# Hybrid decoder trunk, gated linear attention: ScalarE's two level copies move ahead of the next chunk's decays

## The chip, the core and the metric

One core of a Trainium2 chip runs the whole program. The time is the device time of one execution, in microseconds (us); three executions of the kernel before gave 2348.33, 2348.94 and 2350.07 us, so the median is 2348.94 us.

The core has five engines that run side by side, each with its own instruction list, worked off in order. TensorE (PE in the profile) multiplies matrices and writes to PSUM; VectorE (DVE) and ScalarE (ACT) read and write SBUF and PSUM; GpSimd (POOL) works on SBUF here; SyncE (SP) issues the transfers. They meet by semaphores: an instruction that waits holds up everything behind it on its own engine.

## The reference

Two layers. Each layer normalises x, projects it to the inputs of four mixers and a gate, runs the mixers, multiplies by SiLU(gate), projects back and adds to x. SEQ is 1024 and D_MODEL 1024. The change is inside mixer A, gated linear attention (GLA), with 8 heads, 32 key channels and 64 value channels a head:

```python
def step(S, inp):
    q_, k_, v_, g_ = inp
    G = jnp.cumsum(g_, axis=2)
    o_inter = jnp.einsum('bhtk,bhkv->bhtv', q_ * jnp.exp(G), S)
    diff = G[:, :, :, None, :] - G[:, :, None, :, :]
    decay = jnp.exp(jnp.where(causal, diff, -jnp.inf))
    A = jnp.sum(q_[:, :, :, None, :] * k_[:, :, None, :, :] * decay, axis=-1)
    o = o_inter + jnp.einsum('bhts,bhsv->bhtv', A, v_)
    G_last = G[:, :, -1:, :]
    S_new = jnp.exp(G_last[:, :, 0, :])[..., None] * S + jnp.einsum('bhsk,bhsv->bhkv', k_ * jnp.exp(G_last - G), v_)
    return S_new, o
```

The output o then gets an RMSNorm over each head's 64 channels. The scores A inside a chunk carry a decay for each key channel, so they are no plain product of q and k.

## The kernel before

**Tiling of the mixer.** The kernel works in 8 chunks of 128 tokens (TT = 8). The 128x128 causal triangle of a chunk is cut in 7 levels: level 1 is the one 64x64 block below the diagonal, level 2 the two 32x32 blocks, and so on to 64 blocks of one element at level 7; the diagonal itself comes from a plain product of k and q. Within a level a block's decay splits into a factor for the keys and one for the queries, both exponentials of differences to G at the block's edge. The levels go in three batches, (1, 2), (3, 4, 5) and (6, 7) (`BATCHES`).

**What each engine does for chunk c** (a step that I call mix c, c = 0 to 7):

- VectorE, `mix_dve`: `exponent(c + 1)`, 14 subtractions (lines 737 and 738) that write the exponents of the next chunk into one of the two halves of the buffer gla_E; then `mask_batch(c, 0)`, whose one instruction (line 787) writes the diagonal, and with it all of gla_A, after it has waited for the output of chunk c - 1 (`out_done`); `state(c - 1)` (lines 823 and 826); `means(c - 1)` (lines 832 and 833), which waits for ScalarE's squares; `mask_batch(c, 1)`, three masked copies (line 797) of levels 3 to 5; `normalise(c - 1)` (line 837); `mask_batch(c, 2)`, two masked copies (line 797) of levels 6 and 7.
- ScalarE, `mix_act`: `copy_k_end(c - 1)` (line 880); `decay(c + 1)`, four exponentials (lines 862, 865 and twice 867) that wait for `exponent(c + 1)` and release GpSimd's products of the next chunk; `move_level(c, 1)` and `move_level(c, 2)`, three plain copies in all (line 809) from PSUM into gla_A, which wait for line 787 (the semaphore `masked`) and count up the semaphore `moved`; `square(c - 1)` (line 886); `root(c - 1)` (lines 890 and 891), which waits for the means.
- TensorE, `mix_pe`: `scores(c, 0)` (lines 767 and 774), which waits for all of chunk c - 1's masked copies; `finish(c - 1)` (lines 916, 924, 927 and 937), the output and the state of the chunk before; `scores(c, 1)` (line 774, 48 matmuls), which waits for `moved` of this chunk, since its results go over the same PSUM columns; `scores(c, 2)` (line 774, 32 matmuls), which waits for the masked copies of levels 3 to 5. After each of the three parts stand 10 matmuls (line 255) of other projections, put there by `units_between`.
- GpSimd, `chunk_pool(c + 1)` in the time of mix c: after `decay(c + 1)` it multiplies q and k with the decays (lines 707 and 709), batch by batch, and each batch first waits until TensorE has done the same batch of chunk c (`scored`); line 724 makes the last two products. In chunks 0, 1, 3, 4, 6 and 7 it also does a quarter of a weight tile's low part (line 209) after the second batch and another one at the end.

All orders are written out by hand; there is no planner. After mix 7 TensorE goes on with the gate projections of the same mixer. `scalar_gla` calls `mix_act` for c = 0 to 7, with evacuations of the projections in between, once in each layer.

Of the kernel before, what the change touches and what calls it, by code (L numbers as in the profile page):

```python
# [559 lines left out]
class Gla:  # L560
# [332 lines left out]
    def mix_act(self, act, link, c):  # L893
        if c >= 1:
            self.copy_k_end(act, c - 1)
        if c + 1 < TT:
            self.decay(act, c + 1)
        self.move_level(act, c, 1)
        self.move_level(act, c, 2)
        if c >= 1:  # L900
            self.square(act, c - 1)
            self.root(act, link, c - 1)
# [2096 lines left out]
```

## Time and profile before

| what | value |
|---|---|
| median of three executions | 2348.94 us |
| the profiled execution's own time | 2350.63 us |
| its span in the profile | 2348.8 us |
| TensorE busy | 2266.7 us (97%) |
| VectorE busy | 1130.9 us (48%) |
| GpSimd busy | 920.6 us (39%) |
| ScalarE busy | 895.8 us (38%) |
| the eight mixes of layer 0 | about 118 to 248 us of the span |
| the eight mixes of layer 1 | about 1280 to 1411 us of the span |

Busy time is the sum of an engine's instructions. The chain of waits follows the work that ended last back through what released it. A row of the timeline gives start, duration, engine, line, operation, output<-inputs, shapes and count; in square brackets stands how long the engine was idle before it, and what ended the idle time.

### The profile page before, as it was taken

How to read it: one execution, taken by the hardware profiler on the slowest of the kernel's cores; microseconds unless marked ns; L12 is line 12 of the kernel's file. 1: busy time of each engine (PE TensorE's matmuls, PEld its weight loads, DVE VectorE, ACT ScalarE, POOL GpSimd, SP SyncE). 2: the span in 40 equal slices, each digit the busy share in tenths (PEclk: the TensorE clock that was granted, in tenths of full speed). 3: DMA queues.
4: the chain of work that ended last, by engine and by line, in shares of the span. 5: the costliest groups of instructions: out<-in, count | busy, mean ns of one | idle time of the engine just before them, and what ended most of it. 6: DMA issues, size and time to landing. Idle time of an engine off the chain costs nothing.

```text
span 2348.8 us, 35114 instructions
## 1 busy us (share of the span) xinstructions
PE 2266.7 (97%) x14164; PEld 1737.2 (74%) x14164; DVE 1130.9 (48%) x2214; ACT 895.8 (38%) x1496; POOL 920.6 (39%) x978
## 2 busy tenths in 40 slices
PE   7989999999999999999999899999999999999999
PEld 7877888986595785655697778889866958866556
DVE  4377243634427225767433771446153371277763
ACT  5333225613424433353443332156143343344441
POOL 2166113223724511565433542122245245017563
PEclk9999999999999999999999999999999999999999
DMA  4100232240100111300421003322301001122003
GB/s 158 41 20 20 91 112 90 73 144 1 36 20 1 52 48 65 135 1 1 145 73 40 20 20 91 137 65 90 126 1 37 19 1 52 59 78 111 1 1 135
DMA packets 92018, 141.30 MB, mean 60 GB/s; under 512 B 18352, under 2 KB 65488, under 8 KB 91856
## 3 DMA queue, kind: packets, MB, share of 16 engines
q1 hardware_dynamic: 91856, 139.05, 17.3%
q8 instruction: 113, 1.85, 0.3%
q14 instruction: 49, 0.40, 0.1%
HBM read 105.48 MB, written 33.55 MB: 59 GB/s over the span
## 4 chain that ended last, share of the span: by engine, by line
PE 86%; DVE 9%; ACT 3%; issue 2%; POOL 0%; DMA 0%; SPq 0%; ACTq 0%; DVEq 0%
PE psum L255 40%; PE psum L524 15%; PE psum L1442 6%; PE psum L1425 4%; PE psum L1404 3%; PE psum L1430 3%; PE psum L1428 3%; PE psum L1390 3%; PE psum L774 2%; DVE gla_A L797 2%; PE psum L1449 1%; DVE gla_E L737 1%; PE psum L1042 1%; PE psum L1828 1%; DVE mla_nm L1563 1%
## 5 line engine op out<-in xcount | busy, mean ns | idle before, releaser
L209 POOL TENSOR_TENSOR w_lo<-w_raw,w_hi 128x512 fp32r<-128x512 f32 (+3 forms) x240 | 320.3, 1360 | 757.0 <-ACT w_hi L194 757.0
L255 PE MATMUL psum<-h_hi,w_hi 128*128 128x512 f32 x768 | 203.9, 406 | 0.0
L255 PE MATMUL psum<-h_hi,w_lo 128*128 128x512 f32 x768 | 196.8, 396 | 0.0
L255 PE MATMUL psum<-h_lo,w_hi 128*128 128x512 f32 x768 | 195.2, 394 | 0.0
L194 ACT ACTIVATE w_hi<-w_raw 128x2048 fp32r<-128x2048 f32 (+2 forms) x64 | 114.5, 1788 | 184.1 <-PE psum L524 161.7
L255 PE MATMUL psum<-w_hi,h_hi 128*128 128x256 f32 (+3 forms) x1280 | 183.6, 286 | 0.0
L1637 POOL TENSOR_TENSOR mla_acc<-mla_acc,mla_p 128x512 f32<-128x512 f32 (+3 forms) x160 | 153.5, 977 | 74.1 <-ACT mla_p L1496 74.1
L255 PE MATMUL psum<-w_lo,h_hi 128*128 128x256 f32 (+3 forms) x1280 | 179.4, 283 | 0.0
L255 PE MATMUL psum<-w_hi,h_lo 128*128 128x256 f32 (+3 forms) x1280 | 179.4, 283 | 0.0
L1637 POOL TENSOR_TENSOR fox_acc<-fox_acc,fox_p 128x512 f32<-128x512 f32 (+3 forms) x160 | 150.7, 960 | 73.1 <-ACT fox_p L1496 72.7
L255 PEld LDWEIGHTS psum<-w_hi,h_hi 128*128 128x128 f32 x1280 | 165.4, 192 | 6.0 <-issue 5.8
L255 PEld LDWEIGHTS psum<-h_hi,w_hi 128*128 128x128 f32 x768 | 143.5, 193 | 32.4 <-issue 3.0
L255 PEld LDWEIGHTS psum<-h_hi,w_lo 128*128 128x128 f32 x768 | 144.6, 190 | 30.9
L255 PEld LDWEIGHTS psum<-h_lo,w_hi 128*128 128x128 f32 x768 | 143.7, 189 | 31.0
L255 PEld LDWEIGHTS psum<-w_lo,h_hi 128*128 128x128 f32 x1280 | 164.7, 191 | 0.1
L255 PEld LDWEIGHTS psum<-w_hi,h_lo 128*128 128x128 f32 x1280 | 164.7, 191 | 0.0
L1496 ACT ACTIVATE mla_p<-psum 128x512 f32<-128x512 f32 (+1 forms) x192 | 93.9, 490 | 153.5 <-PE psum L1432 115.7
L1496 ACT ACTIVATE fox_p<-psum 128x512 f32<-128x512 f32 (+1 forms) x192 | 94.2, 490 | 152.4 <-PE psum L1432 114.3
L557 DVE TENSOR_TENSOR x_rows<-x_rows,psum 128x512 f32<-128x512 f32 x128 | 86.0, 686 | 130.4 <-PE psum L524 103.9
L707 POOL TENSOR_TENSOR gla_E<-gla_kT,gla_E 128x128 f32<-128x128 f32 x112 | 54.0, 482 | 151.0 <-ACT gla_kT L643 66.9
L797 DVE COPY_PREDICATED gla_A<-gla_masks,psum 128x512 f32<-128x512 int32 x80 | 77.4, 968 | 30.0 <-PE psum L774 27.5
L1404 PE MATMUL psum<-mla_k,mla_q 128*128 128x512 f32 (+1 forms) x192 | 73.9, 422 | 11.8 <-DVE mla_nm L1567 7.5
(333 smaller groups left out, 4426.2 us busy)
## 6 DMA issues: line engine op xcount, KB each, us to landing
w_raw<-in_w_in_dram SPq DMA_DIRECT2D x38, 1024.0 KB, 5.4
out_dram<-x_rows SPq DMA_DIRECT2D x64, 512.0 KB, 2.7
x_rows<-out_dram SPq DMA_DIRECT2D x56, 512.0 KB, 5.3
w_raw<-in_w_out_dram SPq DMA_DIRECT2D x16, 1024.0 KB, 6.3
x_first<-in_x_dram SPq DMA_DIRECT2D x8, 512.0 KB, 7.3
x_rows<-in_x_dram SPq DMA_DIRECT2D x8, 512.0 KB, 5.3
w_raw<-in_w_in_dram SPq DMA_DIRECT2D x2, 1088.0 KB, 10.0
w_raw<-in_w_in_dram SPq DMA_DIRECT2D x2, 1056.0 KB, 5.1
```

What stands on the lines that cost most here:

```text
L194: last = act.activation(self.w_hi[c["set"]][:, at], self.w_raw[c["set"]][:, at], ACT.Copy)
L209: last = pool.tensor_tensor(self.w_lo[c["set"]][:, at], self.w_raw[c["set"]][:, at], self.w_hi[c["set"]][:, at].bitcast(F32), ALU.subtract)
L255: last = pe.matmul(o, lhs, rhs, start=(kk == 0 and n == 0), stop=(kk == KT - 1 and n == 2))
L524: last = pe.matmul(k.bank(u), y, w[:, c, :], start=(c == 0 and i == 0), stop=(c == CT - 1 and i == 2))
L557: dve.tensor_tensor(at, at, ps, ALU.add).then_inc(k.evac_sem["dve"], 1)
L797: dve.copy_predicated(self.halves(self.A[:, :, :], level)[:, :, :, 1, :], m, ps).then_inc(self.masked.sem, 1)
L1390: last = pe.transpose(k.psum[:D, self.misc_bank("pre", p, g), x * P:(x + 1) * P], src(a, 4 * c + x), k.ident[:, :])
L1404: pe.matmul(out, q[:, a, x * P:(x + 1) * P], kk[:, a, :hi - lo], start=True, stop=True).then_inc(self.scores.sem, 1)
L1425: pe.matmul(out, self.k_hi[ks][:, a, keys], self.q_lo[qs][:, a, lo:], start=True, stop=False)
L1442: pe.matmul(self.k.psum[a * HEAD:(a + 1) * HEAD, 4 + i % 2, lo:], self.pairs[p]["v"](a, kb), self.p[:, u % self.PR, lo:], start=(kb == 0), ...
L1496: act.activation(self.p[:, u % self.PR, lo:], self.k.psum[:, u % 2, lo:], ACT.Exp).then_inc(self.exp_done.sem, 1)
L1637: pool.tensor_tensor(acc, acc, p, ALU.add).then_inc(self.acc_done.sem, 1)
```

## The change

Three calls of `mix_act` change places. For every chunk, `move_level(c, 1)` and `move_level(c, 2)` now stand ahead of `decay(c + 1)` in ScalarE's list. No instruction is added or taken away, no wait changes its condition, and the other engines' lists stay as they are.

```diff
     def mix_act(self, act, link, c):
         if c >= 1:
             self.copy_k_end(act, c - 1)
+        self.move_level(act, c, 1)
+        self.move_level(act, c, 2)
         if c + 1 < TT:
             self.decay(act, c + 1)
-        self.move_level(act, c, 1)
-        self.move_level(act, c, 2)
         if c >= 1:
             self.square(act, c - 1)
             self.root(act, link, c - 1)
```

## Rows read from the trace of the kernel before

**Rows 1.** The page's chain of waits: shares of the span by line.

```profile
PE psum L255 40%; PE psum L524 15%; PE psum L1442 6%; PE psum L1425 4%; PE psum L1404 3%; PE psum L1430 3%; PE psum L1428 3%; PE psum L1390 3%; PE psum L774 2%; DVE gla_A L797 2%; PE psum L1449 1%; DVE gla_E L737 1%; PE psum L1042 1%; PE psum L1828 1%; DVE mla_nm L1563 1%
```

**Rows 2.** Windows: stretch, length, busy (count) PE, PEld, DVE, ACT, POOL; clock, DMA.

```profile
100.00:256.00 156.00, 143.33 (x1647) 117.89 (x1646) 107.65 (x221) 53.57 (x106) 76.45 (x140) 0.98 0.05 15
256.00:560.00 304.00, 304.00 (x1607) 256.57 (x1606) 114.94 (x147) 110.84 (x141) 80.35 (x59) 1.00 0.29 98
1262.00:1419.00 157.00, 145.86 (x1648) 119.66 (x1647) 107.22 (x221) 53.87 (x106) 76.39 (x140) 0.97 0.05 15
1419.00:1700.00 281.00, 281.00 (x1491) 237.64 (x1491) 106.16 (x117) 104.88 (x132) 68.30 (x51) 1.00 0.31 106
```

**Rows 3.** Timeline of ScalarE in mix 3, layer 0, and the next mix's first decay.

```profile
173.40 1.70 ACT L862 ACTIVATE gla_E<-gla_E 128x1792 f32<-128x1792 f32 x1 [2.19 <-DVE gla_E L738]
...
175.31 0.68 ACT L867 ACTIVATE gla_E<-gla_G,gla_end 128x128 f32<-128x128 f32 x2
175.90 1.22 ACT L809 ACTIVATE gla_A<-psum 64x512 f32<-64x512 f32 x3
177.15 0.60 ACT L886 ACTIVATE gla_v<-psum 128x512 f32<-128x512 f32 x1
...
189.66 1.71 ACT L862 ACTIVATE gla_E<-gla_E 128x1792 f32<-128x1792 f32 x1 [2.16 <-DVE gla_E L738]
```

**Rows 4.** Timeline of VectorE in mix 3.

```profile
173.50 1.23 DVE L787 TENSOR_TENSOR gla_A<-psum,ident 128x1024 f32<-128x1024 f32 x1
...
177.78 0.69 DVE L832 TENSOR_REDUCE gla_ms<-gla_v 128x8 f32<-128x512 f32 x1 [1.94 <-ACT gla_v L886]
...
178.81 2.23 DVE L797 COPY_PREDICATED gla_A<-gla_masks,psum 128x512 f32<-128x512 int32 x3
...
182.37 2.72 DVE L797 COPY_PREDICATED gla_A<-gla_masks,psum 128x512 f32<-128x512 int32 x2 [0.75 <-PE psum L774]
```

**Rows 5.** Timeline of TensorE in mix 3: the second and third batch of scores.

```profile
177.17 1.57 PE L774 MATMUL psum<-gla_ql,gla_E 32*128 32x64 f32 x48 [0.93 <-ACT gla_A L809]
...
181.18 1.12 PE L774 MATMUL psum<-gla_ql,gla_E 32*128 32x64 f32 x32
```

**Rows 6.** Timeline of GpSimd in mix 3: starts of batches 1 and 2, both weight quarters.

```profile
176.12 0.46 POOL L707 TENSOR_TENSOR gla_E<-gla_kT,gla_E 128x128 f32<-128x128 f32 x1 [5.13 <-ACT gla_E L867]
...
178.85 0.47 POOL L707 TENSOR_TENSOR gla_E<-gla_kT,gla_E 128x128 f32<-128x128 f32 x1 [1.03 <-PE psum L774]
...
181.35 1.27 POOL L209 TENSOR_TENSOR w_lo<-w_raw,w_hi 128x512 fp32r<-128x512 f32 x1
...
185.94 1.31 POOL L209 TENSOR_TENSOR w_lo<-w_raw,w_hi 128x512 fp32r<-128x512 f32 x1
```

**Rows 7.** Timeline of VectorE and GpSimd at the end of mix 0.

```profile
130.02 6.89 DVE L737 TENSOR_TENSOR gla_E<-gla_G 128x128 f32<-128x128 f32 x1
...
135.44 1.32 POOL L209 TENSOR_TENSOR w_lo<-w_raw,w_hi 128x512 fp32r<-128x512 f32 x1
```

**Rows 8.** Timeline of VectorE and ScalarE in mix 2.

```profile
158.24 1.23 DVE L787 TENSOR_TENSOR gla_A<-psum,ident 128x1024 f32<-128x1024 f32 x1 [1.38 <-PE psum L927]
...
159.50 1.24 ACT L809 ACTIVATE gla_A<-psum 64x512 f32<-64x512 f32 x3
...
162.55 2.25 DVE L797 COPY_PREDICATED gla_A<-gla_masks,psum 128x512 f32<-128x512 int32 x3 [0.26 <-PE psum L774]
```

**Rows 9.** Timeline of TensorE and VectorE in mix 1.

```profile
143.34 2.84 PE L774 MATMUL psum<-gla_ql,gla_E 32*128 32x64 f32 x48 [5.68 <-ACT gla_A L809]
...
146.25 2.26 DVE L797 COPY_PREDICATED gla_A<-gla_masks,psum 128x512 f32<-128x512 int32 x3 [1.41 <-PE psum L774]
...
149.65 1.12 PE L774 MATMUL psum<-gla_ql,gla_E 32*128 32x64 f32 x32
```

**Rows 10.** Windows: a stretch of mix 1; columns as in rows 2.

```profile
144.00:150.00 6.00, 6.00 (x66) 4.92 (x66) 3.57 (x6) 1.06 (x3) 2.55 (x6) 0.64 0.00 0
```

**Rows 11.** Timeline of GpSimd in mix 4: start of the third batch.

```profile
198.67 0.53 POOL L707 TENSOR_TENSOR gla_E<-gla_kT,gla_E 128x128 f32<-128x128 f32 x1 [1.02 <-PE psum L774]
```

## Prediction, made before the changed kernel ran

> **What bounds the kernel now.** I read the page's chain first: it is TensorE nearly throughout, and only at the GLA lines do others appear, DVE L797 with 2% and DVE L737 with 1% of the span [rows 1]. So whatever a mix of GLA loses, TensorE loses. The windows say the same and how much room there is. In the 156 us around the eight mixes of layer 0 TensorE is busy for 143.33, so it stands for 12.7 us; in layer 1 for 157 - 145.86 = 11.1; in the stretches that follow (304 and 281 us) it is busy for all of it [rows 2]. A delay of the last mix is therefore carried to the end of the kernel one to one, and a gain too, up to those 24 us.
>
> Then I read one mix of each kind as a timeline. Mix 3 is the regular one. Call T the start of its first decay, 173.40; the next one starts at 189.66, a period of 16.26 us [rows 3]. The chain through it is:
> - decays T to T+2.59 (the last ends at 175.31 + 0.68), moves to T+3.72, squares T+3.75 to T+4.35 [rows 3];
> - second batch of scores on TensorE from T+3.77 to T+5.34, after 0.93 us idle for the moves; third batch from T+7.8 to T+8.9 [rows 5];
> - GpSimd starts batch 1 with the decays at T+2.72, is done with it at 177.82, waits 1.03 us for the second scores, starts batch 2 at T+5.45, and from there to the end of its second weight quarter (185.94 + 1.31 = 187.25, T+13.85) it never stops: 8.40 us [rows 6];
> - VectorE ends its last masked copy at 182.37 + 2.72 = T+11.69 [rows 4], but the 14 subtractions that follow are done only at about 189.6: 2.4 us after GpSimd's last instruction. That VectorE stands still while GpSimd runs is plain in mix 0: a subtraction that takes 0.28 elsewhere took 6.89 us, from 130.02 to 136.91, and GpSimd's last quarter ended at 136.76 [rows 7].
>
> So the period is 5.45 + 8.40 + 2.41 = 16.26: decays, moves, second scores, GpSimd's unbroken stream, rest of the subtractions.
>
> **The change, part by part.** It removes no work. It puts 1.22 us of moves ahead of 2.59 us of decays [rows 3]. Two things come earlier or later by that.
>
> *Moves.* They need line 787, which runs 173.50 to 174.73 [rows 4], so they can start at T+1.37 and end at T+2.6 where they now end at T+3.72. TensorE was idle only from 176.24 (177.17 - 0.93), so the second scores start at T+2.9 and are 0.9 us earlier; they end at T+4.45.
>
> *Decays.* They now run T+2.6 to T+5.2, 2.6 later. Behind them on ScalarE stand the squares, to T+5.8 (1.45 later), and the root. Released by them are GpSimd's next chunk and, through the squares, VectorE's means, and both are in front of what sets the period:
> - GpSimd: start T+5.3 (0.13 after the decays, as now); batch 1 takes 177.82 - 176.12 = 1.7, to T+7.0. The second scores are long there, so it doesn't wait, and the same 8.40 us end at T+15.4 instead of T+13.85. Rest of the subtractions 2.4: next T at T+17.8. Period +1.5.
> - VectorE: means from T+5.85 to T+6.75 (177.78 to about 178.67 now, 0.9), masked copies of batch 1 (2.23) to T+9.0; third scores T+9.1 to T+10.2 (now T+7.8 to T+8.9, TensorE waits some 2.15 us before them); last masked copies end at T+12.95 instead of T+11.69. That is +1.25 by itself.
>
> The 0.9 us that the scores gain is used by nobody: masked copies of batch 1 stand behind the means, GpSimd's batch 2 behind its late batch 1.
>
> By mix:
> - Mix 0: line 787 is the later of the two conditions now too; the moves stay where they are, and the decays, 3.8 us later, are done before GpSimd has finished chunk 0. 0.
> - Mix 1: the one gain. TensorE has been idle for 5.68 us at 143.34 for the moves [rows 9], and starts 1.3 earlier (2.59 of decays less 1.23 of line 787 and its hop). Means end at about 146.15, as late as the 146.25 at which the masked copies start now, so these hardly move; the third scores, at 149.65 now behind ten matmuls at a lowered clock, are then bound by 146.2 + 2.25, at 148.5. -1.2.
> - Mix 2 and mix 5: line 787 waited 1.38 us for the output matmuls and ended at 159.47 = X; the moves start at 159.50 either way, since the decays lay wholly beside that wait [rows 8]. Here nothing is earlier, and the decays move from before X to X+1.27 to X+3.87. Squares to X+4.5, means to X+5.4; masked copies start then instead of at 162.55 = X+3.08: +2.35 on VectorE's path. GpSimd: batch 1 to X+5.65 where batch 2 starts at X+3.1 now, +2.5 to its end. +2.5 each.
> - Mix 3: +1.5 as above.
> - Mix 4: GpSimd has no quarters and already waits 1.02 us for the third scores [rows 11]; it starts later with a stop less, and the third scores' +1.25 counts. +1.25.
> - Mix 6: no subtractions follow; VectorE's last masked copy opens the next scores. +1.25.
> - Mix 7: no decays, 0, and it passes on what it gets.
>
> Sum for a layer: -1.2 + 2.5 + 1.5 + 1.25 + 2.5 + 1.25 = +7.8. Layer 1 has the same lists and nearly the same windows [rows 2]; I take +7.6 there, since TensorE's wait in its mix 1 is a little different. Total +15.4. On the profiled execution's own time: 2350.63 + 15.4 = 2366.0. That execution lies 1.7 us over the median of the runs shown, so in their terms 2348.94 + 15.4 = **2364.3 us**.
>
> *What the trace does not show, from both sides.* How much of the subtractions slips in while GpSimd runs. Now three of 14 do, at the joints of its last instructions; the late stream meets VectorE at the same offset (12.95 against 15.4, before 11.69 against 13.85), so I keep 2.4. If all 14 wait, as the first one did for 6.89 us [rows 7], that is 0.6 more in the three mixes of a layer that follow a stream with quarters: +3.6 in all; if GpSimd never held VectorE, only VectorE's own +1.25 and +2.35 count, and the sum is 7.5 a layer at most, less 0.3 to 1. The Trainium skill ("SBUF — State Buffer", section "Who interferes with whom") says that a VectorE instruction with two SBUF inputs and a GpSimd instruction that reads SBUF exclude each other, and that the one holding the port keeps it for its whole instruction. The trace agrees that they exclude each other; but 6.89 us is many GpSimd instructions of 0.46 to 1.3 us, so the hold here can last a whole stream. By the page's unit, the end of an instruction, the sum would stay at +15.4; by the long hold it is +19.
>
> The other unknown is TensorE's clock. After the idle 5.68 us of mix 1 the granted clock of 144 to 150 us was 0.64, and 48 matmuls took 2.84 us where they take 1.57 at the full 2.4 GHz [rows 5, 9, 10]. After gaps of 0.93 it did not fall. The new order makes gaps of 2.15 us before the third scores in five mixes a layer. From nothing to about 1 us each (1.12 us of scores at half clock) is +0 to +10; I take 0, nearer to the 0.93 row. In mix 1 the gap shrinks to 4.3 us, which may save a microsecond.
>
> **The rivals.**
> - *The early scores pay, and the decays hide* (faster). If GpSimd's idle 5.13 us before a chunk were real slack and the squares cost nothing, mixes 3, 4 and 6 would gain 0.93 each and mix 1 1.2: 4.0 a layer, 2348.9 - 8 = 2341. For it: TensorE waits for the moves in the chain. Against it: GpSimd's stream runs unbroken into the subtractions [rows 6], and the squares are behind the decays on the one list. It decides at whether batch 2 on GpSimd (T+5.45) starts later than now.
> - *It evens out* (within the noise): gains in mixes 1, 3, 4, 6 against losses of mixes 2 and 5 only: -8 + 10 = +2, 2351. It needs the regular mixes to gain, against the same two rows.
> - *Worse than the sum*: the long hold, with some lowered clocks: +19 to +25, 2368 to 2374.
>
> **How the numbers follow.** Forecast 0.76; worse than the sum 0.14; evens out 0.04; faster 0.06. This kernel's runs tell a difference of about 0.2%, 4.7 us, from none. Slower 0.90, same 0.04, faster 0.06. Range: the forecast's own bounds are about +12 (VectorE's path alone, a better mix 1) to +19; with part of the worse case +23: 2358 to 2372.
>
> **What would show it.** In the changed profile the moves (L809) end before L862 starts; scores x48 start about 2.9 us after the subtractions; GpSimd's first L707 of a chunk comes 5.3 us after them, with no stop before batch 2; L832 starts 1.4 to 2.6 later and L797 x3 directly behind it; periods near 17.8 for mix 3, 16.3 for mix 4; the eight mixes end near 256 instead of 248 us; TensorE is 8 us longer idle in each layer, with gaps in front of L774 x32 released by L797. If L862 after mix 3 comes 16.3 us or less after the one before, the prediction is wrong.

## The result, and the profile after

The changed kernel took 2382.91 us, median of four executions (2379.53 to 2390.78), against 2348.74 us before: the ratio is 1.0149, 95% interval 1.0124 to 1.0175. Slower, as forecast, but by 34 us where I had said 15.4, and outside my range (2358 to 2372). Timed once more beside the last experiment it gave 1.0146 (1.0127 to 1.0165).

The profiled execution has a span of 2377.7 us, 28.9 more than before. First the windows of the changed kernel that answer to [rows 2] (stretch, length, busy and count of PE, PEld, DVE, ACT, POOL, then granted clock, DMA share, GB/s):

```profile
150.00:263.00 113.00, 101.26 (x1182) 82.33 (x1181) 73.53 (x144) 35.19 (x72) 49.84 (x92) 0.89 0.04 11
263.00:290.00 27.00, 27.00 (x133) 22.68 (x132) 3.62 (x6) 8.08 (x11) 5.03 (x4) 1.00 0.53 157
290.00:560.00 270.00, 270.00 (x1443) 228.63 (x1442) 104.47 (x114) 99.67 (x126) 69.98 (x52) 1.00 0.27 95
```

After the mixes TensorE is busy without a stop, as before. But inside them the granted clock has a mean of 0.89, where it was 0.98 over the whole of that stage [rows 2], and 1.00 in mixes 2 to 6 alone (150 to 238 us of the kernel before). That is new, and it is where the missing time is. Mix 3 of the changed kernel, timeline of ScalarE (answers to [rows 3]):

```profile
176.26 1.24 ACT L809 ACTIVATE gla_A<-psum 64x512 f32<-64x512 f32 x3 [3.54 <-DVE gla_A L787]
177.52 1.70 ACT L862 ACTIVATE gla_E<-gla_E 128x1792 f32<-128x1792 f32 x1
179.43 0.68 ACT L867 ACTIVATE gla_E<-gla_G,gla_end 128x128 f32<-128x128 f32 x2
180.14 0.60 ACT L886 ACTIVATE gla_v<-psum 128x512 f32<-128x512 f32 x1
```

VectorE (answers to [rows 4]) and TensorE (to [rows 5]) in the same mix:

```profile
175.00 1.22 DVE L787 TENSOR_TENSOR gla_A<-psum,ident 128x1024 f32<-128x1024 f32 x1 [0.88 <-PE psum L927]
180.77 0.69 DVE L832 TENSOR_REDUCE gla_ms<-gla_v 128x8 f32<-128x512 f32 x1 [3.44 <-ACT gla_v L886]
181.57 2.18 DVE L797 COPY_PREDICATED gla_A<-gla_masks,psum 128x512 f32<-128x512 int32 x3
177.72 1.57 PE L774 MATMUL psum<-gla_ql,gla_E 32*128 32x64 f32 x48
183.81 1.78 PE L774 MATMUL psum<-gla_ql,gla_E 32*128 32x64 f32 x32 [2.02 <-DVE gla_A L797]
191.01 1.01 PE L774 MATMUL psum<-gla_ql,gla_E 32*128 32x64 f32 x32
```

Read it from the top: line 787 ends at 176.22, the moves follow at once, the decays, the squares, and VectorE's means wait 3.44 us for the squares. The three masked copies start only behind the means, though their scores were done at 179.3. TensorE has then waited 2.02 us ahead of the third scores, and from there it is slow: 1.78 us for the 32 matmuls, and the chain of waits shows the ten matmuls of other projections (line 255, called the product matmuls from here on) on the path behind them, at nearly twice their usual 2.5 us:

```profile
183.81 1.78 PE psum L774 x32
185.59 4.56 PE psum L255 x10
190.16 1.02 PE psum L767 x16
```

From the start of the third scores to the start of the next mix's x32 it is 191.01 - 183.81 = 7.20 us. In the kernel before it was 4.51 in the same mix, from 181.18 [rows 5] to this row of its timeline:

```profile
185.69 1.02 PE L774 MATMUL psum<-gla_ql,gla_E 32*128 32x64 f32 x32
```

That interval is a good gauge of the clock, since where the granted clock is 1.00 it is 4.5 us. In mixes 2 to 6 of the changed kernel it is 5.63, 7.20, 5.67, 5.65 and 7.21 in layer 0, and 5.67, 4.50, 5.65, 7.21 and 5.66 in layer 1. What lies over 4.5 adds to 8.9 + 6.2 = 15.1 us. The span grew by 28.9; without that it would have grown by 13.8, where the sum was 15.4. Counted from line 787 of mix 0 to line 787 of mix 7, the mixes of the two layers took 117.8 and 118.5 us before and take 134.2 and 132.0 now: 29.9 more, and 14.8 without the 15.1.

Mix 1 stands apart. TensorE waits less there than before, 2.94 us instead of 5.68, and the 48 matmuls run at full speed; the eight product matmuls behind them, which take 2.0 us elsewhere, are slow all the same, and the granted clock of 141 to 147 us is 0.72:

```profile
141.04 1.57 PE L774 MATMUL psum<-gla_ql,gla_E 32*128 32x64 f32 x48 [2.94 <-ACT gla_A L809]
142.53 3.30 PE L255 MATMUL psum<-h_hi,w_lo 128*128 128x512 f32 x8
```

That fall costs little, since the third scores wait for the masked copies there anyway, by 0.92 us. It shows that a first row at full speed does not yet mean a full clock.

### The profile page after: what moved, and what is told of

Its sections match the earlier page's. It is cut to its first block, busy times and chain, and to the rows that moved or that the text cites. A ratio compares the mean times of both kernels' runs of the same rounds, so it can differ in the third digit from the quotient of the medians.

```text
span 2377.7 us, 35114 instructions
## 1 busy us (share of the span) xinstructions
PE 2283.8 (96%) x14164; PEld 1749.4 (74%) x14164; DVE 1131.7 (48%) x2214; ACT 896.4 (38%) x1496; POOL 917.6 (39%) x978
## 4 chain that ended last, share of the span: by engine, by line
PE 84%; DVE 9%; ACT 4%; issue 2%; POOL 0%; DMA 0%; SPq 0%; DVEq 0%; ACTq 0%
PE psum L255 39%; PE psum L524 15%; PE psum L1442 6%; PE psum L1425 4%; PE psum L1404 3%; PE psum L1430 3%; PE psum L1428 3%; PE psum L1390 3%; DVE gla_A L797 2%; PE psum L774 2%; PE psum L1449 1%; PE psum L1042 1%; PE psum L1828 1%; PE psum L927 1%; DVE mla_nm L1563 1%
## 5 line engine op out<-in xcount | busy, mean ns | idle before, releaser
L255 PE MATMUL psum<-h_lo,w_hi 128*128 128x512 f32 x768 | 202.3, 404 | 0.0
L774 PE MATMUL psum<-gla_ql,gla_E 32*128 32x64 f32 x1792 | 62.4, 281 | 32.9 <-DVE gla_A L797 24.7
L774 PEld LDWEIGHTS psum<-gla_ql,gla_E 32*128 32x128 f32 x1792 | 57.2, 195 | 46.2 <-DVE gla_A L797 31.5
```

What stands on the lines that cost most here:

```text
L255: last = pe.matmul(o, lhs, rhs, start=(kk == 0 and n == 0), stop=(kk == KT - 1 and n == 2))
L774: last = pe.matmul(out[:, i, g, :], self.E[r, c % 2, level - 1, g, :], self.ql[r, level - 1, g, :], start=True, stop=True)
```

## The experiments

Ratios are to the kernel before on the same chip in the same rounds. Its median was 2347.95 us beside four of the kernels (after filled, squares first, squares late, after with quarters moved), 2351.66 beside the next four (after filled in mixes 2 to 6, before with quarters moved, split decays, squares first with quarters moved) and 2349.27 beside the last two.

**After, filled.** TensorE gets something to do in the wait:

```diff
         between(pe, 1)
+        if 1 <= c < TT - 1:
+            name, part = unit_between(BETWEEN * (self.NBATCH * c + 2) // UNIT_MATMULS)
+            bank = self.k.bank(self.k.u(self.layer, name, *part))
+            for i in range(8):
+                pe.matmul(bank[:64, :P], self.k.upper[64:, :64], self.k.ident[64:, :], start=False, stop=False,
+                          skip_group_check=True)
         self.scores(pe, c, 2)
```

> The changed kernel, with 8 matmuls more in mixes 1 to 6 on TensorE, right ahead of the third batch of scores. They multiply zeros into the open accumulation of the projection that runs there (64 rows, 64x128 of it), so nothing that is computed changes; at about 0.21 us each they fill 1.7 of the 2.0 us that TensorE waits there in the changed kernel. Theory A (clock): that wait drops TensorE to its lower clock, and the scores (1.78 us for 32 matmuls where 1.12 is usual) and the ten product matmuls behind (4.56 where 2.5 is usual) are on the path. Then the filling gives the time back: 2364 to 2368 us, the granted clock of 150 to 260 us near 1.0 instead of 0.89. Theory B (something else makes these matmuls slow, or the serial chain of diagonal, moves, decays, squares, means and masks alone costs the 34 us): no change or slower, 2380 to 2390 us.

Measured: 2369.42 us, ratio 1.0086 (1.0069 to 1.0103), against the changed kernel's 1.0149: more work on TensorE, and some 13 us less. Its mix 3:

```profile
183.74 1.96 PE L952 MATMUL psum<-ident,upper 64*64 64x128 f32 x16
186.31 1.12 PE L774 MATMUL psum<-gla_ql,gla_E 32*128 32x64 f32 x32 [0.61 <-DVE gla_A L797]
190.83 1.02 PE L774 MATMUL psum<-gla_ql,gla_E 32*128 32x64 f32 x32
```

The interval is 4.52 again in this mix, and 4.5 in eight of the ten (mix 6 of both layers has 5.64); the granted clock of 150 to 250 us is 0.98 instead of 0.88. So the matmuls were slow by the clock, and it was TensorE's standing still at this place that made it fall so often. 2369.4 is a little over the 2364 to 2368 expected; each of the 8 became two instructions of the array, 1.96 us in all, and in mix 1, where there is hardly a wait, the filling was pure cost.

**After, filled in mixes 2 to 6.** `if 1 <= c` becomes `if 2 <= c`.

> The filled kernel of before (zeros on TensorE ahead of the third scores), filled in mixes 2 to 6 only. In mix 1 there was next to no wait to fill, and its period was 19.98 us instead of the 17.71 of the changed kernel. Theory: the clock cost of the changed kernel is all in mixes 2 to 6, and what is left without it is the delay of the serial chain as I predicted it, +15.4 us. Then 2363 to 2366 us. If the filling itself costs more than that in the other mixes, or the chain costs more than predicted: 2368 us and more.

Measured: 2369.55 us beside 2351.66, ratio 1.0074 (1.0057 to 1.0090), that is +17.9 us. Three of its ten intervals were still 5.65 to 5.68 us, 3.5 us in all, though only 0.5 to 0.6 us of waiting was left ahead of them. What is left of the 17.9, about 14, is what the late decays and squares cost by themselves. The time is over the 2363 to 2366 expected, by about those three falls.

**Squares first.** The changed order, with `square(c - 1)` between the moves and the decays.

```diff
         self.move_level(act, c, 2)
+        if c >= 1:
+            self.square(act, c - 1)
         if c + 1 < TT:
             self.decay(act, c + 1)
         if c >= 1:
-            self.square(act, c - 1)
             self.root(act, link, c - 1)
```

> The changed kernel with the squares (L886) ahead of the decays too: moves, squares, decays, root. VectorE's means come as early as before the change or earlier, so TensorE should not wait ahead of the third scores; the decays stay late, by 0.6 us more than in the changed kernel. Theory A (the clock drop comes of the late squares): about +15 us over the kernel before, from GpSimd's late stream alone, 2362 to 2368 us. Rival: the late stream makes the subtractions late, TensorE then waits 2 to 3 us for the moves instead, and the clock falls there: 2375 us or more. If neither late squares nor late decays cost much by themselves: under 2356.

Measured: 2352.65 us, ratio 1.0016 (1.0007 to 1.0025). The decays are later than in the changed kernel, and nearly all of the 34 us is gone. The starts of line 787 give the mixes' periods in layer 0: 16.71, 17.24, 17.58, 15.12, 17.23 and 15.11 us for mixes 1 to 6, where the kernel before has 18.77, 15.26, 16.28, 16.27, 15.33 and 16.25. So late decays do cost 1.3 to 2.0 us in mixes 2, 3 and 5, those where GpSimd has its quarters in the stream; but early moves with early squares win 1.1 in mixes 4 and 6 and 2.1 in mix 1, and it nearly evens out. (The profiled execution, 2349.19 us, is one of the two fastest of ten; the median lies 3.5 us above it.) My expectation of +15 from GpSimd's stream alone was wrong. The rival had a part of it: in mix 3 of both layers TensorE waits 1.8 us for the moves, and the granted clock of 172 to 184 us is 0.86; but GpSimd's stream is the longer path there, and the time came out under 2356.

**Squares late.** The old order, with only the squares held back:

```diff
         self.move_level(act, c, 2)
         if c >= 1:
+            if c + 1 < TT:
+                for i in range(7):
+                    link(act.activation(self.k.ss[:, :], self.end_16[:, 0, :], ACT.Copy))
             self.square(act, c - 1)
```

> The kernel before, order as it was, with seven tiny linked activations (8 elements a row, about 0.24 us each, 1.7 us together; they write a row-sum tile that nothing reads later) between the moves and the squares in mixes 1 to 6. Decays, GpSimd's stream and moves stay on time; only the squares, and so the means and the masked copies behind them, are late by 1.7 us. Theory A (late squares open the gap ahead of the third scores, and the clock falls there): 1.6 us of delay and 1 to 2 us of slow matmuls a mix, 2375 to 2388 us. Without a clock effect: 12 mixes times 1.6 = +19, 2367. If GpSimd's stream alone sets the period: under 2356 us.

Measured: 2362.12 us, ratio 1.0059 (1.0044 to 1.0074), 14 us over the kernel before, with decays and moves at their old places. Mix 3, all from its timeline:

```profile
177.19 1.65 ACT L903 ACTIVATE norm_ss<-gla_end 128x8 f32<-128x8 f32 x7
178.87 0.60 ACT L886 ACTIVATE gla_v<-psum 128x512 f32<-128x512 f32 x1
182.81 1.12 PE L774 MATMUL psum<-gla_ql,gla_E 32*128 32x64 f32 x32 [1.51 <-DVE gla_A L797]
187.30 1.02 PE L774 MATMUL psum<-gla_ql,gla_E 32*128 32x64 f32 x32
```

Squares late by 1.65 us make TensorE wait 1.51 us for the masked copies and lengthen the mixes to 16.5 and 17.7 us. Here the clock fell in none of the ten places (intervals 4.49 to 4.53, granted clock 1.00 from mix 2 to mix 6 in both layers), and the run came out where I had put it without a clock effect, 2367, or below. The late squares alone are worth what the whole delay of the changed kernel was to be.

**After, quarters moved.** GpSimd's weight quarters leave its streams:

```diff
     def chunk_pool(self, pool, c, between):
...
+        if c in (2, 4, 5):
+            pool.wait_ge(self.exponents.sem, self.exponents.at(c + 1))
+            between(pool)
+            between(pool)
         pool.wait_ge(self.decays.sem, self.decays.at(c + 1))
...
-            if b == 1:
+            if b == 1 and c == 0:
                 between(pool)
...
-        between(pool)
+        for i in range({0: 1, TT - 1: 4}.get(c, 0)):
+            between(pool)
...
```

(c is the chunk here, one more than the mix in whose time it is worked on; the cut at the end is the condition on c at the call, which goes.)

> The changed kernel with GpSimd's weight quarters (L209, 1.3 us each) taken out of its streams in mixes 0, 2, 3, 5: two each go ahead of its wait for the decays in mixes 1, 3 and 4, behind the subtractions, and four to the end of chunk 7. The same work, other places. My prediction had GpSimd's unbroken stream set the period; then this gives back 1.5 us and more in mixes 2, 3 and 5 of each layer, 2370 to 2374 us. If the path is now the serial chain through the output matmuls (L927), the diagonal (L787), moves, decays, squares and means, as the chain of waits of the changed kernel reads: less than 5 us, 2378 to 2383.

Measured: 2373.65 us, ratio 1.0109 (1.0094 to 1.0124), a gain of about 9 us by the medians. By the total that fits the first expectation, but not by its place: mixes 2 to 5 got no shorter. The starts of line 787, which is line 792 in this kernel:

```profile
154.86 1.22 DVE L792 TENSOR_TENSOR gla_A<-psum,ident 128x1024 f32<-128x1024 f32 x1 [1.38 <-PE psum L932]
173.69 1.23 DVE L792 TENSOR_TENSOR gla_A<-psum,ident 128x1024 f32<-128x1024 f32 x1 [2.54 <-PE psum L932]
194.05 1.23 DVE L792 TENSOR_TENSOR gla_A<-psum,ident 128x1024 f32<-128x1024 f32 x1 [3.35 <-PE psum L932]
214.41 1.22 DVE L792 TENSOR_TENSOR gla_A<-psum,ident 128x1024 f32<-128x1024 f32 x1 [3.46 <-PE psum L932]
```

These are 18.83, 20.36 and 20.36 us apart, and the changed kernel had 18.79, 20.09 and 18.81; mix 5 is 18.84 against 18.82. Mix 6 is 18.80 against 20.35, with a milder fall of the clock. All these hold falls. Where the clock stayed up, in mixes 3 and 4 of layer 1, the periods are 17.64 and 17.65 us; the changed kernel has one such mix, with 17.94, and its repeat below has 17.46 in mix 3 and 17.64 in mix 4 of layer 0. In mixes 3 to 6 of layer 0 VectorE now waits 2.0 to 3.5 us for the output matmuls instead of 0.9 to 2.4: the subtractions are done earlier, and nobody needs them. What sets the period is the chain through TensorE. The two profiled executions differ by 5.1 us only (spans of 2372.6 and 2377.7): some 1.3 come from mix 0 of layer 0, where line 787 of mix 1 starts at 137.19 instead of 138.50, about 2.5 from mix 0 of layer 1 (17.15 us against 19.60), and 1.2 from the falls (13.9 us over the ten intervals instead of 15.1). The other 4 of the 9 are between the medians and these executions, and no profile shows them.

**Before, quarters moved.** The same edit to the old order.

> The kernel before with GpSimd's weight quarters out of the streams of mixes 0, 2, 3 and 5, at the same places as in the changed kernel with moved quarters. Theory (in the old order the period of mixes 2, 3 and 5 is set by GpSimd's unbroken stream, as I read it before): each of these gets as short as mix 4, which has no quarters, 15.0 instead of 16.3 us, and mix 0's blocked subtractions start about 1.3 us earlier; together 4 to 6 us a layer, 2337 to 2341 us. If VectorE or TensorE is the limit of these mixes anyway: 2345 to 2349.

Measured: 2338.68 us beside 2351.66, ratio 0.9941 (0.9926 to 0.9955). The mixes 2 to 6 all take 15.3 us (starts of line 787: 156.46, 171.74, 187.04, 202.36, 217.66, 232.94). The three that took 16.3 us (3, 4 and 6, counted from line 787 to line 787; counted from first decay to first decay it was mixes 2, 3 and 5, those with quarters, that took 16.3 to 16.6) lose 1.0 us each, the other two had 15.3 already; mix 1 starts 2.6 us earlier, its subtractions no longer blocked, and gives 0.8 of that back. In layer 1 mix 1 gains as well, 16.50 us against 19.58. The gain of 13 us is more than the 8 to 12 expected. So in the old order GpSimd's unbroken stream did hold the kernel up, as I had read it.

**Split decays.** The level decays ahead of the moves, the other three behind them:

```diff
         if c + 1 < TT:
             self.decay(act, c + 1)
         self.move_level(act, c, 1)
         self.move_level(act, c, 2)
+        if c + 1 < TT:
+            self.decay_ends(act, c + 1)
         if c >= 1:
             self.square(act, c - 1)
...
```

> The order decays of the levels (L862), moves, other three decays, squares; GpSimd's products of the levels wait for L862 alone, its last two products for the other three (one more semaphore). The moves are 1.0 us earlier than in the kernel before, the squares come when they came before, GpSimd starts earlier. Theory (early moves are worth TensorE's 0.9 us of waiting, as long as the squares and GpSimd aren't late): about 0.9 in mixes 1, 3, 4 and 6 of each layer, 2340 to 2343 us. Rival (the moves are never worth anything, since the squares and means bound the masked copies): 2347 to 2350.

Measured: 2352.25 us beside 2351.66, ratio 0.9999 (0.9990 to 1.0009). The rival held in the total. TensorE no longer waits for the moves, but for the masked copies:

```profile
173.99 1.57 PE L775 MATMUL psum<-gla_ql,gla_E 32*128 32x64 f32 x48
178.75 1.12 PE L775 MATMUL psum<-gla_ql,gla_E 32*128 32x64 f32 x32 [0.71 <-DVE gla_A L798]
```

In mixes 3, 4 and 6, where the squares come as long after the diagonal as before (3.6 us), the moves are 1.1 us earlier and the period 0.2 us shorter (16.06 against 16.3). In mixes 2 and 5 the squares were not kept on time: they come 3.6 us after the diagonal instead of 2.5, and the period is 0.8 us longer. With 1.6 us won in mix 1 of layer 0 it evens out.

**Squares first, quarters moved.** Both edits from above together.

> Moves, squares, decays, root, and GpSimd's quarters out of its streams. With moves and squares early and the late decays behind them, the one thing late is GpSimd's chunk, and without quarters its stream is 2.6 us shorter, more than the 2.1 us that it starts late. Theory: faster than both kernels, 2333 to 2340 us. Rival (the late stream still meets the subtractions, and the clock falls in some mix): 2345 or more.

Measured: 2330.63 us beside 2351.66, ratio 0.9909 (0.9894 to 0.9923): faster than both kernels, and 8 us faster than moved quarters alone. Every mix from 2 to 6 takes 15.24 to 15.29 us, and TensorE waits for nothing that matters in them:

```profile
171.45 1.57 PE L779 MATMUL psum<-gla_ql,gla_E 32*128 32x64 f32 x48
175.43 1.12 PE L779 MATMUL psum<-gla_ql,gla_E 32*128 32x64 f32 x32
```

Mix 1 gives 2.9 us of it in layer 0 (16.70 against 19.57) and 1.4 in layer 1 (15.08 against 16.50): in layer 0 TensorE waits 1.80 us for the moves instead of 3.18 and takes 1.57 us for the x48 instead of 2.26, but it doesn't keep its clock, which is 0.72 at 139 to 145 us. Another 3.2 of the 9.9 us between the two profiled executions lie in the last stretch ahead of the mixes of layer 1, where the granted clock is 1.00 instead of 0.92; no run here changes that stretch by itself.

**After, unaltered, and after, filled short.** The second has `range(3)` in place of `range(8)`, in mixes 2 to 6.

> The changed kernel once more, unaltered, beside the short filling below on the same chip. Its first four runs spread from 2379.5 to 2390.8 us where the kernel before spreads by 2 to 4. Theory (how often the clock falls in the ten mixes with the 2 us wait differs from run to run): again a spread of several us around 2380.

> The filled kernel with 3 instead of 8 matmuls of zeros ahead of the third scores, mixes 2 to 6. At about 0.23 us each they take 0.7 us, so that a wait of some 1.6 us stays, where the changed kernel waits 2.0 to 2.4 and the kernel with late squares waited 1.2 to 1.5 with its clock at 1.0. Theory (the length of the idle stretch decides): mostly full clock, 2365 to 2370 us like the kernel with 8. Rival (it was the number of matmuls, or any wait at this place, that decides): between, 2373 to 2383.

Measured: the changed kernel 2384.14 us (2381.02 to 2388.29, ratio 1.0146), the short filling 2374.83 (ratio 1.0103, 1.0086 to 1.0119). In the repeat the same place comes out either way. Three third scores of its layer 0 with the x32 that follows each:

```profile
182.77 1.12 PE L774 MATMUL psum<-gla_ql,gla_E 32*128 32x64 f32 x32 [2.06 <-DVE gla_A L797]
187.26 1.02 PE L774 MATMUL psum<-gla_ql,gla_E 32*128 32x64 f32 x32
218.16 1.12 PE L774 MATMUL psum<-gla_ql,gla_E 32*128 32x64 f32 x32 [2.30 <-DVE gla_A L797]
223.81 1.01 PE L774 MATMUL psum<-gla_ql,gla_E 32*128 32x64 f32 x32
236.95 1.80 PE L774 MATMUL psum<-gla_ql,gla_E 32*128 32x64 f32 x32 [2.27 <-DVE gla_A L797]
244.15 1.01 PE L774 MATMUL psum<-gla_ql,gla_E 32*128 32x64 f32 x32
```

4.49, 5.65 and 7.20 us after waits of 2.06, 2.30 and 2.27. With a wait of 1.5 left, the short filling still has lowered clocks:

```profile
184.20 1.97 PE L774 MATMUL psum<-gla_ql,gla_E 32*128 32x64 f32 x32 [1.55 <-DVE gla_A L797]
191.41 1.01 PE L774 MATMUL psum<-gla_ql,gla_E 32*128 32x64 f32 x32
```

Here the rival of that expectation held: it came between. (The profiled execution is the slowest of its four; its ten intervals lie 15.5 us over 4.5 in all, as much as those of the changed kernel, so that the 9 us between the medians are not seen in it.) The length of the wait just ahead does not decide by itself, since late squares left 1.2 to 1.5 us at the same place ten times without a fall, and the short filling, with 1.3 to 1.6 us, had eight falls in ten; the two fillings by 8 had five in twenty after waits of 0.5 to 0.6, and one wait of 2.08 in the changed kernel had none. What besides does (the filling uses a quarter of the array) stays open.

The repeat also shows that these ten places are not all that differs from run to run. Its ten intervals lie only 11.1 us over 4.5, some 4 less than in the first profile, and its mixes take 25.7 us more than in the kernel before, 14.6 without the falls. Yet its span is 1.5 us longer, since the stretch from the last mix of layer 0 to the first of layer 1 took 1049.5 us instead of 1043.9. A part of that stretch, first in the changed kernel and then in the repeat (columns as in rows 2):

```profile
1003.07:1053.07 50.00, 48.25 (x255) 26.98 (x252) 33.80 (x91) 22.00 (x43) 28.43 (x33) 1.00 0.00 0
998.23:1048.23 50.00, 48.25 (x241) 26.23 (x240) 32.51 (x92) 21.10 (x40) 26.67 (x31) 0.96 0.00 1
```

## Why the prediction was wrong

- *Moves and decays.* Right. The moves start 0.04 us behind line 787, the decays end 2.6 us behind the moves. The second scores came with hardly a wait (177.72 in mix 3), and nobody used it. Splitting the decays agrees: moves 1.1 us earlier were worth 0.2 us in the mixes where nothing else was late, and the ratio is 0.9999.
- *Squares, means, masked copies.* Right, and it is the part that costs: held back alone they cost 14 us, put first they take nearly all of the loss away. In the regular mix 3 I had them as the shorter of two chains, +1.25 beside GpSimd's +1.5; they are the longer.
- *GpSimd's stream.* Right for the kernel before (moved quarters: 0.9941), mis-sized for the changed one. The mechanism is there (1.3 to 2.0 us in mixes 2, 3 and 5 with squares first), but I wrote of it as what sets the new period, and moving the quarters shortened mix 3 by at most 0.3 us and the others not at all.
- *The sum without the clock.* 15.4 against 13.8 us of span by the gauge above, and about 14 by the filled kernel. From line 787 of mix 0 to that of mix 7 it is 14.8, and 14.6 in the repeat. The serial terms, by mix, came out: the filled kernel's mixes 2 to 5 take 17.85, 17.88, 17.68 and 17.86 us, which is +2.6, +1.6, +1.4 and +2.5 where I had +2.5, +1.5, +1.25 and +2.5. There is luck in it: I took GpSimd's stream as the limit in mix 3, and the sum is right only because the squares' chain was priced within 0.25 us of it.
- *TensorE's clock.* This is the step that failed: the term for the clock, which I put at 0. I had the wait (2.15 us ahead of the third scores, five mixes a layer; measured 2.02 to 2.46), and I wrote "From nothing to about 1 us each", "is +0 to +10; I take 0, nearer to the 0.93 row". Measured it was 15.1 us in the profiled execution and 11.1 in that of the repeat: in the first, nine of ten waits brought a fall, at 1.15 us each in six of them and 2.7 in three. Filling the waits took 13.5 us back. Two errors in one. Nothing between 0.93 and the waits with a fall spoke for 0: no row had a wait near 2, and besides the 5.68 of mix 1 the kernel before had one of 4.27 in layer 1 with slow matmuls behind it (row below). And the price counted the 32 score matmuls alone, not the ten product matmuls behind them, which are in front of the next mix's first scores and were up to 2.07 us longer. With the ten counted, the upper end would have been 10 times 2.7 = 27 us, and the range would have reached 2391. The rival that was worse than the sum had some lowered clocks in it, but its 2368 to 2374 is 9 us short of the result too. What in the chip makes a wait of 2 us bring a fall at one time and not at another, no run here shows.

```profile
1305.14 2.58 PE L774 MATMUL psum<-gla_ql,gla_E 32*128 32x64 f32 x48 [4.27 <-ACT gla_A L809]
```

- *The rest of the 34.* The span grew by 28.9, the medians by 34.2: the profiled execution was the fastest of its four (3.4 us under the median), and that of the kernel before was 1.9 over its own. That the slower ones had more or longer falls fits the filled kernels' smaller loss and spread (1.4 and 3.3 us over four runs, against 7 and 11), but their profiles were not taken, and the repeat shows falls outside the ten places too.
- *The range.* Its lower end doesn't follow from its terms: +12 gives 2361, not 2358. That had no part in the miss.
- *The Trainium skill's rule on the port* ("SBUF — State Buffer", section "Who interferes with whom") decided nothing here: three of 14 subtractions slipped in, as before (in mix 3 they start at 188.15, 188.42 and 189.16, and GpSimd's last instruction ends at 190.37).

## What to carry to other kernels

Before moving work ahead of a critical instruction on an in-order engine, follow everything that it pushes back, to the end of each chain; here a 0.6 us square behind the decays, late by 1.5 us and more, cost more than the earlier moves gained. Where an edit opens a new idle stretch on TensorE in a stage that has none of its length, price the lowered clock with all matmuls that follow until the next wait, and put that into the range. An order that doesn't pay alone can pay on top of another change: moves and squares first were +0.16% alone, and -0.3% on top of moved quarters.

## What was not expected of the hardware

The small VectorE instruction behind the reduction (line 833, 8 elements a row, SBUF to SBUF, one input) took 0.17 us in all 16 places before, and 0.43 to 0.45 in ten of 16 in the changed kernel, in mixes 1, 2, 4, 5 and 6 of both layers, where GpSimd is at work beside it. (GpSimd is at work in mix 3 as well, where it took 0.17; why, no run here shows. With squares first, where the means come ahead of GpSimd's chunk, it took 0.17 in all 16.) The same line in the kernel before and then in the changed one (minimum, median, maximum in ns):

```profile
L833 DVE TENSOR_SCALAR gla_ms<-gla_ms x16: 171/172/173, 144.7 to 1419.8; 128x8 f32<-128x8 f32 x16
```

```profile
L833 DVE TENSOR_SCALAR gla_ms<-gla_ms x16: 170/436/453, 145.0 to 1448.8; 128x8 f32<-128x8 f32 x16
```

It stands in the serial chain: from line 787 to the third scores it is 9.08 us in mix 2, where it took 0.45, and 8.81 in mix 3. That is 0.27 us in many mixes that no row of the kernel before could show. The other surprise is that the same wait at the same place brings a lowered clock in one execution and not in the next (mix 3: interval 7.20 in the first profile of the changed kernel, 4.49 in the second), so a kernel at this edge also spreads more: 7 to 11 us over four runs where the kernel before spreads by 2 to 5.
